# Down weights of the third expert: asked for behind its up weights instead of after the first gather

## What is computed

```python
def hier_moe(x, ...):
    lc = t @ rc_w + rc_b;  g_sel = argmax(lc)               # one of 4 groups
    lf_sel = (t @ rf_w + rf_b)[group g_sel]                 # its 8 experts
    top_v, top_i = top_k(lf_sel, 2);  top_w = softmax(top_v)
    ...
        h = silu(t @ w_gate[e]) * (t @ w_up[e]) * gates
        y = y + h @ w_down[e]
```

## Time and profile before

| | |
|---|---|
| runs shown | 712.40, 712.37, 712.54 us |
| profiled execution, its own time | 710.51 us |
| its span | 708.5 us |
| TensorE busy | 675.1 us (95%) |
| VectorE / ScalarE / GpSimd busy | 301.5 / 110.4 / 39.5 us |
| bytes moved | 229.82 MB, mean 324 GB/s |
| granted TensorE clock over the span | 0.982 |

### The profile page before, as it was taken

One profiled execution on the slowest core, in us unless ns is written; L12 is line 12 of the kernel. 1 busy time (PEld: TensorE's weight loads), 2 busy tenths in 40 slices (PEclk: granted clock), 3 DMA queues, 4 the chain that ended last, 5 costly groups with the idle time before them and its releaser, 6 DMA issues.

```text
span 708.5 us, 8872 instructions
## 1 busy us (share of the span) xinstructions
PE 675.1 (95%) x3792; PEld 375.8 (53%) x3792; DVE 301.5 (43%) x537; ACT 110.4 (16%) x202; POOL 39.5 (6%) x47
## 2 busy tenths in 40 slices
PE   7999999999989999999999999999999999999982
PEld 4999999877865433434434344344343443434331
DVE  5545238513446225323443244333533344324437
ACT  6421243302230000000000000000000000000014
POOL 2000000000002010000100010000000010000000
PEclk9999999999979899999999999999999999999997
DMA  8940600097258799999999999999999999999943
GB/s 285 348 125 3 238 1 1 3 387 295 86 217 318 296 423 417 419 419 419 419 419 420 420 420 418 418 420 420 420 416 419 419 420 420 418 420 421 419 174 133
DMA packets 45227, 229.82 MB, mean 324 GB/s; under 512 B 7844, under 2 KB 15029, under 8 KB 20611
## 3 DMA queue, kind: packets, MB, share of 16 engines
q1 hardware_dynamic: 42627, 224.52, 78.5%
q0 software_dynamic: 2560, 4.73, 1.9%
HBM read 228.03 MB, written 4.85 MB: 329 GB/s over the span
## 4 chain that ended last, share of the span: by engine, by line
PE 72%; SPq 15%; DVE 6%; DMA 5%; ACT 1%; issue 1%; DVEq 0%
PE ps L1455 21%; PE ps L1292 13%; PE ps L1474 12%; SPq L473 10%; PE ps L1363 8%; PE ps L1485 7%; SPq L479 5%; DMA w<-in_moe_w_up 4%; PE ps L1445 2%; DVE x_sb L802 2%; PE ps L1389 1%; PE ps L1431 1%; PE ps L1465 1%; PE ps L1256 1%; PE ps L1258 1%
## 5 line engine op out<-in xcount | busy, mean ns | idle before, releaser
L1455 PE MATMUL ps<-w,xT 128*64 128x512 f32 x1024 | 225.5, 592 | 0.2 <-DMA w<-in_moe_w_up 0.2
L1455 PEld LDWEIGHTS ps<-w,xT 128*64 128x64 f32 x1024 | 73.2, 137 | 147.2 <-issue 143.9
L802 DVE TENSOR_TENSOR x_sb<-ps,x_sb 128x512 f32<-128x512 f32 (+1 forms) x170 | 107.9, 681 | 59.6 <-PE ps L1363 32.8
L1474 PE MATMUL ps<-wd,hexT 128*64 128x512 f32 x512 | 119.1, 608 | 8.3 <-DVE hexT L1147 8.3
L802 DVE TENSOR_TENSOR hexp<-silu_g,ps 128x256 f32<-128x256 f32 x32 | 13.5, 421 | 180.7 <-ACT silu_g L764 180.7
L1474 PEld LDWEIGHTS ps<-wd,hexT 128*64 128x64 f32 x512 | 34.5, 139 | 73.3 <-issue 62.0
L1485 PE MATMUL ps<-y_hi,home 64*128 64x512 f32 (+1 forms) x320 | 67.7, 419 | 2.2 <-DVE y_lo L808 1.6
L1485 PE MATMUL ps<-y_lo,home 64*128 64x512 f32 (+1 forms) x320 | 63.1, 390 | 0.0
L768 ACT ACTIVATE y_hi<-ps,gate_of 128x512 fp32r<-128x512 f32 x32 | 22.0, 687 | 231.8 <-PE ps L1474 231.8
L808 DVE SCALAR_TENSOR_TENSOR y_lo<-ps,gate_of,y_hi 128x512 fp32r<-128x512 f32 x32 | 24.0, 750 | 69.3 <-ACT y_hi L768 69.3
L573 POOL DMA_INDIRECT xg<-hn_rows,idx x32 | 32.2, 1008 | 380.0 <-PE ps L1445 361.9
(11 more groups left out here) (205 smaller groups left out, 591.2 us busy)
## 6 DMA issues: line engine op xcount, KB each, us to landing
w<-in_moe_w_gate SPq DMA_DIRECT2D x64, 1024.0 KB, 21.1
w<-in_moe_w_up SPq DMA_DIRECT2D x64, 1024.0 KB, 24.2
wd<-in_moe_w_down SPq DMA_DIRECT2D x64, 1024.0 KB, 21.1
wo<-in_w_out SPq DMA_DIRECT2D x2, 2048.0 KB, 11.0
x_sb<-in_x_prompt SPq DMA_DIRECT2D x4, 512.0 KB, 8.8
hn_rows<-hn2p SPq DMA_DIRECT2D x4, 512.0 KB, 2.8
out<-x_sb SPq DMA_DIRECT2D x4, 512.0 KB, 2.6
wi_v<-in_w_in SPq DMA_DIRECT2D x4, 384.0 KB, 8.0
```

The costliest lines, as they stand in the source:

```text
L802: return nc.vector.tensor_tensor(out, a, b, op)
L1455: last = mm(ps[64 * h:64 * h + 64, 1, :], lhs, w1[s][:, :, k, h * (F // 2):(h + 1) * (F // 2)], start=(k == 0), stop=(k == KD - 1))
L1474: last = mm(ps[64 * h:64 * h + 64, 3, :], lhs, wd[s][:, c, h * 512:(h + 1) * 512], start=(c == 0), stop=(c == F // P - 1))
```

## The change

The two DMAs of expert 2's down weights move up on SP's queue: from behind the wait for the first gather to right behind the last up weights of expert 2, ahead of `row_ids`. The wait of SP for the first gather goes; nothing else is changed.

```diff
             load_gate_up(2, 2, parts=(1,), halves=(1,))
+            load_down(2, 2)
             sp.wait_ge(L_ready, NT)
             sp.dma_start(row_ids[:], consts[:, NKEPT:NCONST]).then_inc(rows_in, 16)
-            sp.wait_ge(xg_in[0], 16)
-            load_down(2, 2)
```

## The result

The changed kernel takes 715.01 us (median of 10 runs, 714.1 to 716.46); the kernel before, in runs beside it, 712.38 us (10 runs, 711.39 to 714.16). The ratio is 1.0035, 95% interval 1.0024 to 1.0045: 2.6 us slower, against a forecast of 3.3 (715.7 us, range 712.0 to 717.4). The profiled execution took 714.67 us, 4.2 us more than that of before; its span is 712.8 us, 4.3 more.

What follows compares the result with a forecast made beforehand. From about 248 us DMA engines and TensorE are both full, starting at the end of expert 0's down products; 1.5 us late gather plus 1.8 us low clock, 3.3 us, takes 712.4 to 715.7 us, range 712.0 to 717.4.

Steps and rivals of the forecast that it cites:

- The gather: First gather of expert 0's rows, issued at 217.84 us: 6.4 us instead of 3.7, bounds 3.7 to 8.2.
- `row_ids` costs nothing: Table load behind the early down weights: some 5 us later, covered by over 10 us, so 0.
- whatever moves the end of expert 0's down products moves all that follows by the same amount: After about 243 us DMA engines and TensorE are both full, so a shift there reaches the kernel's end unchanged.
- The wait: TensorE before the transposes of expert 0's rows, from 222.74 us: 1.5 us late, bounds 0 to 3.3.
- the fourth gather: Gather issued at 224.10 us while these same down weights moved: 5.9 us, taken as a near case.
- My point for the emptying of the queue: SP's queue, with 2.10 MB more, empties 5.0 us later, near 223.7 us instead of 218.7.
- The clock: TensorE's clock falls behind the wait, slowing expert 0's gate and up products by 1.8 us; late gather with low clock, chance 0.47.
- The rival that it holds: At expert 0's transposes the gather is late but the clock stays up: only 1.5 us lost, 713.9 us, chance 0.30.
- The rival that the early issue is covered: First gather still lands in time, within 4.9 us, nothing on the path moves: 712.4 us, chance 0.13.

Runs made afterwards that it cites:

- e4: The changed kernel with the `row_ids` table and its wait back ahead of the down loads on SP's queue; ratio 1.0059 to the kernel before.
- e3: The kernel before with three extra matmuls of unread result ahead of the transposes of expert 0's rows, no DMA moved; ratio 1.0033 to the kernel before.
- e7: The kernel before with the 30 narrow matmuls of turn 0 moved behind expert 0's down products; ratio 0.9976 to the kernel before.
- e2: The changed kernel with three extra matmuls of unread result ahead of the transposes of expert 0's rows; ratio 1.0020 to the kernel before.
- e5: The changed kernel run once more without an edit, beside later runs of the kernel before; ratio 1.0054 to the kernel before.
- e1: The kernel before with only the first of expert 2's two down loads (1 MiB of 2) issued early; ratio 1.0023 to the kernel before.
- e6: The changed kernel with 2 MiB of expert 2's gate and up weights made to wait for the first gather instead; ratio 1.0003 to the kernel before.
- e9: The kernel before with the edits of e7 and e8 together; 709.67 us, ratio 0.9974 to the kernel before.
- e8: The kernel before with two matmuls of unread result in TensorE's 1.99 us pause at 198.8 us; ratio 0.9980 to the kernel before.

## Why the prediction came out as it did

**The direction and the mechanism were right.** The gather is the term that decides, it comes behind a full queue, TensorE waits at the first transposes, the clock falls with the wait, `row_ids` costs nothing (e4), and the delay goes through to the end (e3; 4.23 us at SP's issue, 4.3 in the span). One sentence of it is too strong: that whatever moves the end of expert 0's down products moves all that follows by the same amount. It holds for a delay of TensorE; in e7 that end came 7.2 us earlier, with work of TensorE moved behind it, and the kernel gained 1.7.

**The gather was put too low.** I took 6.4 us between two rows, 5.9 and 6.8. It took 7.2 to 7.3 us in all four profiles that have the 2 MiB early (the change, e2, e4, e5). The wait was 2.49 us instead of 1.5, still inside the bounds of 0 to 3.3. This term was mis-sized by the choice of the fourth gather as a near case: at its issue SP's queue had moved 0.20 of the 2.10 MB asked for at 221.55, so 1.9 MB were left, where the first gather of the change has 2.44 MB beside it. My point for the emptying of the queue was too early as well, 223.7 against about 225: until the first gather landed the engines moved 2.40 MB of SP's queue and 0.44 MB of the gathers, and the sum has SP's loads alone. In the change the gather lands just as the queue runs dry.

**The clock was put about right, and its price varies.** 1.8 us forecast; 1.40 in the first profile, 1.4 by e2 against the change, 2.34 in e5. That it would fall was given 0.47 against 0.30, and it fell in all three profiles of kernels with the full wait. The rival that it holds leaned on the Trainium skill ("TensorE: Matmul & The Clock Gate", section "Why this matters for your kernels"). The runs disagree with that rule as it stands: the clock fell behind a wait of 0.82 us (e1) and with no wait at all (e6). What these cases have in common is narrow matmuls just before. But the same matmuls stand before the 0.77 us of e9 and before the transposes of the kernel before, where the clock held, so when it falls is not settled here.

**That the sum came so near is in part luck.** In the first profile the two misses partly cancel (2.49 + 1.40 = 3.9 us against 1.5 + 1.8 = 3.3), in e5 both terms came out above the forecast, 4.8 us together. The timed runs lost 2.6 us beside the first runs of before, 3.8 and 4.2 beside the later ones (e5, e4, by the ratio). Part of this spread is the kernel before's own. Of the 76 runs of it beside the experiments, 22 have a granted clock of 0.979 or less over the span, and their median span is 710.4 us; 43 have 0.981 or more, with 708.9. Both profiles of before (0.982 and 0.981, 708.5 and 709.2 us) belong with the second group. In which stretch the clock fell in the other runs is not on record. e6 shows that it can fall at 222 us without a wait; a run of before in which it does has paid part of the clock term already. That this is what happens is argued, not shown.

**The rival that the early issue is covered** (the Trainium skill, "DMA: Bandwidth & Descriptors", section "Rules for kernel authors", by which the setup cost of a DMA overlaps when it is issued early and waited for late) falls with the 7.3 us: nobody waits for the loads themselves, but the gather issued while they drain is late, and TensorE waits for that.

## What to carry to other kernels

A load that nobody waits for is not free to issue early: ask which small transfer, on whatever queue, is issued while it drains, and who waits for that one. A wait on the issuing queue that looks idle can be what keeps the DMA engines clear for such a transfer; the slack to compare it with is that of the small transfer, here 1.2 us against a delay of 3.6.

When a wait on TensorE is priced, look at what it did before: behind narrow matmuls even a short wait can go with a fall of the clock (0.82 us in e1 did, 0.77 us in e9 did not), and the price, 1.4 to 2.3 us here, is then paid by the dense work behind it.

## What the runs showed of the hardware that I had not expected

One indirect gather of 128 rows of 2 KB took 3.2 to 4.2 us where SP's queue was running dry at its issue, 5.7 with 1 MiB more queued and 7.2 to 7.3 with 2 MiB more, although the two are different queues. Its first packet moved 1.9 to 2.1 us after the issue in the kernel before and 4.3 to 4.5 in the changed one.

TensorE's clock fell from 1.00 to 0.50 while TensorE was busy (e6 at 222 us, and every kernel here in or right behind the 30 narrow matmuls of turn 0). And the same wait does not always cost it: behind 2.6 us it fell in e8 and held in e9.
